# Part of the recurrence's elementwise work on GpSimd and ScalarE in place of VectorE

## The reference

```
xx = shift(h) - h
xr, xw, xk, xv, xa, xg = [h + xx * mix[i] for i in range(6)]
r, k, v = xr @ w_r, xk @ w_k, xv @ w_v
decay = exp(-exp(-softplus(-(w0 + tanh(xw @ w1) @ w2)) - 0.5))
a = sigmoid(a0 + (xa @ a1) @ a2)
kk = k * k_k;  kk = kk / norm(kk, per head)
k = k * (1 + (a - 1) * k_a)
for each token t and each of 16 heads of 64:
    S = S * decay_t - (S kk_t) (kk_t * a_t)^T + v_t k_t^T
    y_t = S r_t
y = group_norm(y) + (sum(r * k * r_k)) * v;  return (y * sigmoid(xg @ g1) @ g2) @ w_o
```

## Time and profile before

| what | value |
| --- | --- |
| timed runs | 2705.49 us median, 2704.85 lowest, 2709.05 highest |
| profiled execution | span 2706.4 us, first to last instruction; no other time is listed for it |
| TensorE busy | 2380.3 us, 88% of the span |
| VectorE busy | 1862.4 us, 69% |
| ScalarE busy | 1218.7 us, 45% |
| GpSimd busy | 622.8 us, 23%, nearly all of it gathers before 1565 us |
| projections of the time mix | end at 2349.3 us |
| triangular inverse | 2386.53 to 2418.83 us |

### The profile page before, as it was taken

How to read it: one execution, slowest core, us unless ns; L and a number is a source line. 1 busy time by engine, 2 the same in 40 slices (tenths; PEclk the granted TensorE clock), 3 DMA queues, 4 the chain that set the end, 5 groups by cost and what they waited for, 6 DMA issues and landing times. The chain is left out here.

```text
span 2706.4 us, 35151 instructions
## 1 busy us (share of the span) xinstructions
PE 2380.3 (88%) x12882; PEld 1586.5 (59%) x12882; DVE 1862.4 (69%) x3462; ACT 1218.7 (45%) x2588; POOL 622.8 (23%) x529
## 2 busy tenths in 40 slices
PE   6988788888888988888778799999999998977999
PEld 4774334333334444343333268898888887866887
DVE  4767866677667867867765666676667666797665
ACT  3433434444444544444434454457445444534543
POOL 0003444554444434455544400000000000000000
PEclk9988999999999999999999999999999998977999
DMA  9789999999999999999999945542555554212553
GB/s 386 257 329 423 403 427 427 424 427 424 424 411 418 376 426 411 427 427 427 427 424 426 427 160 186 186 156 98 183 186 181 188 188 165 91 50 111 179 187 116
DMA packets 121706, 811.27 MB, mean 300 GB/s; under 512 B 15713, under 2 KB 18825, under 8 KB 26584
## 3 DMA queue, kind: packets, MB, share of 16 engines
q0 software_dynamic: 74160, 540.05, 47.7%
q1 hardware_dynamic: 47400, 269.32, 27.5%
HBM read 807.12 MB, written 1.15 MB: 299 GB/s over the span
## 5 line engine op out<-in xcount | busy, mean ns | idle before, releaser
L1402 PE MATMUL bank<-rows,diag 128*128 128x512 f32 (+1 forms) x2060 | 995.9, 620 | 212.6 <-ACT diag L1559 212.1
L1797 DVE CUSTOM_DVE_ANT_0 rows<-rows,h 128x1024 f32<-128x1024 f32 (+1 forms) x512 | 620.3, 1224 | 359.7 <-DMA rows<-in_peer_rows,idx 353.3
L1402 PEld LDWEIGHTS bank<-rows,diag 128*128 128x128 f32 (+1 forms) x2060 | 371.8, 194 | 739.7 <-ACT diag L1559 421.1
L1281 POOL DMA_INDIRECT rows<-in_peer_rows,idx x512 | 609.0, 1189 | 741.5 <-PE bank L1402 679.3
L1550 ACT ACTIVATE picks<-picks 128x1 f32<-128x1 f32 (+1 forms) x512 | 103.3, 202 | 637.9 <-DVE picks L1797 617.5
L2142 PE MATMUL bank<-hT_pair,halves 128*128 128x512 f32 x864 | 307.2, 399 | 0.4 <-DVE hT_pair L2020 0.4
L2143 PE MATMUL bank<-hT_pair,halves 128*128 128x256 f32 x864 | 242.2, 280 | 0.0
L1559 ACT ACTIVATE diag<-const_table,picks 128x128 f32<-128x128 f32 (+1 forms) x512 | 205.5, 401 | 48.0 <-ACT picks L1554 1.1
L2076 DVE TENSOR_TENSOR halves<-weight_ring,halves 128x2048 fp32r<-128x2048 f32 x74 | 169.3, 2289 | 74.3 <-ACT halves L2071 74.1
L2142 PEld LDWEIGHTS bank<-hT_pair,halves 128*128 128x128 f32 x864 | 162.3, 188 | 40.9 <-DVE hT_pair L2020 0.9
L1314 PE MATMUL bank<-halves_b,halves_a 128*128 128x256 f32 x912 | 172.0, 331 | 0.0
(11 more groups left out here) (571 smaller groups left out, 3772.2 us busy)
## 6 DMA issues: line engine op xcount, KB each, us to landing
weight_ring<-in_ffn_w_gate SPq DMA_DIRECT2D x44, 1024.0 KB, 4.7
weight_ring<-in_ffn_w_up SPq DMA_DIRECT2D x44, 1024.0 KB, 4.8
weight_ring<-in_ffn_w_down SPq DMA_DIRECT2D x44, 1024.0 KB, 4.8
mod_ring<-in_mod_w SPq DMA_DIRECT2D x16, 1024.0 KB, 7.5
weight_ring<-in_peer_w_q SPq DMA_DIRECT2D x16, 1024.0 KB, 11.3
half_ring<-in_mod_w SPq DMA_DIRECT2D x24, 512.0 KB, 7.2
rows<-in_mod_w SPq DMA_DIRECT2D x12, 1024.0 KB, 8.1
weight_ring<-in_attn_w_in SPq DMA_DIRECT2D x12, 1024.0 KB, 4.7
```

The source lines that it names most:

```text
L1281: nc.gpsimd.indirect_dma_start(ring[:, s], None, dram["peer_rows"], bass.IndirectOffsetOnAxis(ap=idx[:, T, n:n + 1], axis=0)).then_inc(row ...
L1402: mm = nc.tensor.matmul(bank[:, :], diag[0:n, j % DIAG_SLOTS], ring[0:n, j % ROW_SLOTS, D + half * 512:D + (half + 1) * 512], start=(j in ...
L1797: dotted.up(nc.vector.tensor_tensor_reduce(out=ring[r, s, 0:D], in0=ring[r, s, 0:D], in1=its_h, scale=1.0, scalar=0.0, op0=ALU.mult, op1=A ...
```

## The change

1. In `project_mixes` SP also loads the row k_a (`ka_row`), into the other half of the slot that holds `kk_row`. GpSimd, once both raw removal keys are made, computes for each tile `rated_part = K * ka_row` and `K = K - rated_part`, in that slot.
2. In `wkv` GpSimd multiplies `rated_part` by the rate A, adds it to K, and multiplies K by `down`; VectorE loses `key_factor`, `key` and both products K * down. `rate_key`, which overwrites A, waits for GpSimd's product.
3. VectorE adds the biases of L for both tiles, then those of A.
4. ScalarE copies all grams from PSUM unmasked, between its copies of the turned halves. GpSimd masks GK in SBUF, one instruction for a tile, and then the right half of GA. The inverse reads the left half of GA unmasked, in entries above the diagonal only.
5. The semaphores follow: TensorE's next use of a bank waits for the copy, the products with GK for GpSimd's mask, the shares of GA for the third mask. VectorE's transpose waits for the copies of GA and for GpSimd's K * down, whose input and output it would otherwise overtake.

```
+        @block.gpsimd                       # in project_mixes
+        def _(pool):
+            pool.wait_ge(made.sem, NT)
+            for T in range(NT):
+                kit.pool(nc.gpsimd.tensor_tensor(rated_part[:, T], K[:, T], ka_row, ALU.mult))
+                kit.pool(nc.gpsimd.tensor_tensor(K[:, T], K[:, T], rated_part[:, T], ALU.subtract))
...
+            for T in range(NT):             # in wkv, GpSimd
+                pool.wait_ge(rated.sem, NT + T + 1)
+                key_rated.up(gtt(rated_part[:, T], rated_part[:, T], A[:, T], ALU.mult))
+            for T in range(NT):
+                pool.wait_ge(key_rated.sem, T + 1)
+                kit.pool(gtt(K[:, T], K[:, T], rated_part[:, T], ALU.add))
+                pool.wait_ge(exped.sem, 5 * T + 4)
+                k_scaled.up(gtt(Kd[:, T], K[:, T], down[:, T], ALU.mult))
...
+            pool.wait_ge(rows_in.sem, 32)
+            for T in range(NT):
+                pool.wait_ge(grams_out.sem, 2 * NT + 2 * T + 2)
+                masked.up(mask(GK[:, T * RH:(T + 1) * RH, :], P, 2 * C))
+            masked.up(mask(GA[:, :, C:], P + 3 * C, C))
...
+            place_next(5)                   # in wkv, ScalarE
+            copy_grams(GA, 0, 0)
+            copy_grams(GA, 1, 2)
+            place_next(2)
+            copy_grams(GK, 0, 6)
+            place_next(2)
+            copy_grams(GK, 1, 0)
...
-            key_factor(0)                   # in wkv, VectorE
             rate_key(0)
             scale_r(0)
             scale_keys(0)
-            key_factor(1)
             rate_key(1)
             scale_r(1)
             scale_keys(1)
-            key(0)
             place_half(3)
-            k_scaled.up(tt(Kd[:, 0], K[:, 0], down[:, 0], mul))
-            mask(GA, P + 2 * C, grams_a, masked_a, 0, 0)
-            key(1)
             place_half(4)
             place_half(5)
-            k_scaled.up(tt(Kd[:, 1], K[:, 1], down[:, 1], mul))
-            mask(GA, P + 2 * C, grams_a, masked_a, 1, 2)
+            dve.wait_ge(k_scaled.sem, NT)
+            dve.wait_ge(grams_out.sem, 2 * NT)
...
-                if i in (4, 10):
-                    mask(GK, P, grams_k, masked_k, i // 10, 0 if i == 10 else 6)
```

More of the change, by code:

```diff
@@ L163, in dve, with pool @@
         self.nc.vector.wait_ge(self.step["dve"].sem, self.step["dve"].up(ins))
+    def pool(self, ins):
+        self.nc.gpsimd.wait_ge(self.step["pool"].sem, self.step["pool"].up(ins))
     def act(self, ins):
@@ L3240, in _ @@
         def _(sp):
-            for i, row in enumerate((dram["rw_ka_2"], dram["rw_rk_2"].rearrange("e h d -> e (h d)"))):
-                rows_in.up(sp.dma_start(rows[:, i], bcast(row, D)), 16)
+            rows_in.up(sp.dma_start(rows[:, 1], bcast(dram["rw_rk_2"].rearrange("e h d -> e (h d)"), D)), 16)
             rows_in.up(sp.dma_start(chunks[:], dram["chunks"]), 16)
@@ L3305, in flip, with grams @@
                     turned.up(mm)
-            def grams(T, keys, j, bank, columns_of, done):
+            def grams(T, keys, j, bank, columns_of):
                 for half in range(2):
@@ L3314, in grams @@
                     if hh // 2 == KD - 1:
-                        done.up(mm)
+                        grams_made.up(mm)
             for j in range(4):
                 flip(j)
-            grams(0, BT, 2, 0, first_a, grams_a)
+            grams(0, BT, 2, 0, first_a)
             flip(4)
@@ L3322, in _ @@
             pe.wait_ge(innered.sem, 4)
[L3323 removed]
+            grams(1, BT, 5, 2, first_a)
             flip(6)
[L3325 removed]
+            grams(0, KT, 6, 6, block_of)
             flip(7)
[L3327 to L3330 removed]
+            pe.wait_ge(grams_out.sem, 2)
+            grams(1, KT, 7, 0, block_of)
+            pe.wait_ge(grams_out.sem, 4)
             for q in range(4):
@@ L3501, in _, with copy_grams @@
             exp_before(1)
-            place_next(len(on_act) - 4)
+            def copy_grams(G, T, b):
+                for i in range(2):
+                    act.wait_ge(grams_made.sem, grams_out.n + 1)
+                    grams_out.up(nc.scalar.copy(G[:, T * RH + i:(T + 1) * RH:2, :], kit.bank[b + i][:, :].rearrange("p (a t) -> p a t", t=2 * C)))
+            place_next(5)
[5 more added lines that the diff above has]
+            copy_grams(GK, 1, 0)
             for T in range(NT):
@@ L3554, in _ @@
             tt, stt = nc.vector.tensor_tensor, nc.vector.scalar_tensor_tensor
[L3555 to L3559, removed]
             def place_half(j):
@@ L3565, in _ @@
             dve.wait_ge(bias_in.sem, 32)
-            for T in range(NT):
-                for m, dst in enumerate((L, A)):
+            for m, dst in enumerate((L, A)):
+                for T in range(NT):
                     for i in range(2):
@@ L3577, in _ @@
                     biased.up(tt(quarter(before, 2 * T + i), kit.bank[4 + 2 * T + i][:, :], quarter(L, 2 * T + i), ALU.subtract))
[L3578 to L3585, removed]
+            dve.wait_ge(rows_in.sem, 32)
             def rate_key(T):
+                dve.wait_ge(key_rated.sem, T + 1)
                 step(tt(A[:, T], A[:, T], KN[:, T], mul))
@@ L3748, in _, with mask @@
             cleared.up(nc.gpsimd.memset(slot(4)[:, 0:C * C:C + 1], 1.0))
+            gtt = nc.gpsimd.tensor_tensor
+            for T in range(NT):
[6 more added lines that the diff above has]
+                k_scaled.up(gtt(Kd[:, T], K[:, T], down[:, T], ALU.mult))
+            def mask(G, at, n):
+                return gtt(G, G, chunks[:, at:at + n].unsqueeze(1).to_broadcast([P, G.shape[1], n]), ALU.mult)
+            pool.wait_ge(rows_in.sem, 32)
+            for T in range(NT):
+                pool.wait_ge(grams_out.sem, 2 * NT + 2 * T + 2)
+                masked.up(mask(GK[:, T * RH:(T + 1) * RH, :], P, 2 * C))
+            masked.up(mask(GA[:, :, C:], P + 3 * C, C))
             pool.wait_ge(within_out.sem, 4 * NT)
```

18 lines of the change are left out of this document (11 added, 7 removed).

## The result

The changed kernel took 2718.93 us in the median of seven runs (2716.83 to 2720.26), the kernel before 2709.05 in the median of seven beside it (2704.85 to 2714.43). The ratio is 1.0036, with a 95% interval of 1.0025 to 1.0046: slower by 9.9 us. A second group of five runs later gave 2720.23 against 2707.87, ratio 1.0049 (1.0035 to 1.0063).

What follows compares the result with a forecast made beforehand. VectorE was taken as the bound up to the triangular inverse's end. Projections +3.4 and the inverse's end +10.4 (its start +5.3 included) gave +13.8: span 2706.4 to 2720.2, less 0.9, 2719 us (2713 to 2725; 8 in 10: 2704 to 2725).

Steps and rivals of the forecast that it cites:

- What bounds the kernel, and the sign: VectorE bounds up to the triangular inverse's end; holds in turns (chance 0.62) make the change slower (chance 0.72).
- signs that it named: VectorE instructions at 3 us and more, GpSimd's at 3.7, projections' block ending 3 late, three inverse steps stretched by 2.5.
- What it costs VectorE: A VectorE instruction with two SBUF inputs waits out GpSimd's whole tensor-tensor of 2.5 us; bounds were nothing and 2.5.
- Projections' last block: Four GpSimd instructions of 2.5 us alternate with VectorE's split and normalisations; the block's end waits, +3.4 us.
- Low-rank products: TensorE's products after the projections: no term in the sum; a little lower TensorE clock stood only in the range's upper end.
- Ahead of the inverse: Scaling of the keys: first product 2.4 late, four GpSimd slips +10.0, two key factors gone -2.5; ends 9.9 later.
- Up to the inverse's start: From second scaled r through turns and grams: the inverse starts at 2391.8 in place of 2386.53, +5.3.
- The inverse: Two mask pairs leave its 32.3 us, three GpSimd masks hold VectorE 3 x 2.5: 37.4 us, ending +10.4.
- VectorE never held: Rival, chance 0.19: only GpSimd waits; inverse starts and ends 7.5 earlier, own-chunk states limit the gain to -4.9, 2700.6 us.
- second path: Last copies of own-chunk states, 0.6 us behind the inverse; without holds they end at 2414.0, limiting the gain to -4.9.
- Both slowed: Rival, chance 0.12: both engines slow while they meet; at two thirds speed +1.5, 2707 us; at half speed +9.
- VectorE wins every turn: Rival, chance 0.07: GpSimd's first mask waits for the inverse's end; +15, and +3 at the projections, 2724 us.

Runs made afterwards that it cites:

- The clears: Changed kernel with each of GpSimd's thirteen two-input instructions replaced by three write-only clears, values of k and masks lost; 2700.99 us, ratio 0.9975 to the kernel before.
- first half only: Kernel before with only K * ka_row and K - rated_part on GpSimd, rest of k on VectorE; 2.4 us at the block's end, 2.9 in low-rank products.
- the pair of 4.81: In the kernel before plus six idle-time pairings: four two-input VectorE instructions beside a GpSimd tensor-tensor, 1.94 us more than the 2.87 beside a clear.
- the probe: Kernel before plus six pairings in VectorE's idle time, each four VectorE instructions of 512 columns beside one GpSimd instruction of 1024; 2731.09 us, one run.

## Why the prediction was right

The forecast was 2719 and the median is 2718.93, but that closeness is largely luck. The forecast was a change of +13.5 us on a kernel before of 2705.49; beside the changed kernel that one took 2709.05 in seven runs, and the change was +9.9. And within the sum errors cancel: by stages of the first profile the holds were priced 4.0 us too dear in three stages, and the low-rank products and the turn stage came out 4.6 us dearer than reckoned.

*What bounds the kernel, and the sign.* Right. VectorE's path set the end of the inverse, before and after. The step that decided, that the hold works in both directions and in turns, was the one trusted least, and it was taken from gathers that showed only one direction. (The trace of before shows a little of the other direction too, which the prediction's median of 1225 ns hides: in the eight cases in which a gather starts within 0.02 us of VectorE's multiplication, the gather takes 0.94, unheld, and the multiplication 1.24 to 1.28.) The clears show it by the opposite: without the reads the same program is 6.4 us faster by stages than before, with them 12.7 to 14.4 slower. Of the signs that it named, VectorE's instructions are at 3.25 to 3.37 (3 and more), each ending about one VectorE length after a GpSimd one; GpSimd's own are at 3.2 to 3.3, not 3.7; VectorE ends the block 2.4 after the last copy of V, not 3; the three steps are 2.0 longer, not 2.5.

*What GpSimd gets.* 2.5 us was estimated for an instruction, measured 2.34 to 2.49 over all profiles. *What it costs VectorE.* The whole 2.5 was taken; measured 2.01 to 2.15 in eight places, about 0.35 less than GpSimd's own length: VectorE's instruction begins up to 0.3 us into GpSimd's, and is let go 0.14 before its end. This is the term that was mis-sized. It shows at every place where it stood:

*Projections' last block.* Predicted +3.4, measured +2.44: the split is 1.15 longer and the two normalisations 3.60, together 4.75; 2.3 of it went unnoticed, since VectorE had ended 2.6 us ahead of the first low-rank product and now ends 0.3 ahead.

*Low-rank products.* Predicted nothing, measured +2.93 and, in another execution, +1.69. The prediction reckoned with "TensorE's clock, a little lower for its longer wait" only as an end of its range; the block's late end of 2.4 costs 1.7 to 2.9 more. This term was missing from the sum.

*Ahead of the inverse.* Predicted +9.9 (a late start of 2.4, four holds of 2.5, two key factors gone), measured +8.34: the same five holds, 10.45 in all, less 2.5, and 0.4 ahead of the first of them: from the first bias to the first scaled key it is 8.03 in place of 7.63, with two waits of 0.17 for TensorE between the biases of L, which now come first. A kernel with the old order of the biases (first half only) has 7.63 again.

*Up to the inverse's start.* The prediction's +5.3 over both stages means -4.6 in the turn stage; measured -2.98 and -3.54. The reason is TensorE's clock again. While VectorE is held, TensorE waits for it (busy 5.36 of the 10 us up to 2375), and after a wait of 3.86 it runs at the lower level: from 2375.0 to 2386.0 of the changed kernel the clock is 0.50, where the earlier trace rows has 1.00 for the same work. The window, and TensorE's rows from that wait on:

```profile
2375.00:2386.00 11.00, 6.54 (x76) 5.42 (x78) 10.93 (x7) 5.27 (x10) 5.92 (x2) 0.50 0.00 1
```

```profile
2372.25 1.97 PE L3317 MATMUL bank<-const_table,R 128*128 128x128 f32 x8 [3.86 <-DVE R L3606]
...
2383.39 1.97 PE L3317 MATMUL bank<-const_table,R 128*128 128x128 f32 x8 [2.58 <-DVE R L3606]
2385.29 2.06 PE L3325 MATMUL bank<-arT,hT 64*32 64x64 f32 x128
2387.28 1.88 PE L3317 MATMUL bank<-const_table,weight_ring 128*128 128x128 f32 x8
...
2391.47 1.48 PE L3325 MATMUL bank<-arT,turned_keys 64*32 64x64 f32 x128 [0.88 <-DVE arT L3235]
```

The prediction's path from the second scaled r to the inverse can be set against them term by term. The turn and the first grams were taken from rows at the higher level, 1.1 + 1.5, and take 4.0 (2383.33 to 2387.35); two turns with their copies 4.0 in place of 3.4; the second grams, taken from a row at the lower level (2.04) and now at the higher one, 1.6 with the wait ahead of them; ScalarE's copies 1.15 in place of 1.1. Together 10.8 in place of 9.1, which is the 1.6 us missing. In the second profile the level is back earlier, the eight turns behind the grams take 1.32 in place of 1.88, and the stage is shorter by the same 0.56:

```profile
2386.63 1.32 PE L3317 MATMUL bank<-const_table,weight_ring 128*128 128x128 f32 x8
```

*The inverse.* Predicted +5.1 (three holds of 7.5 less 2.4), measured +3.64: 6.10 less 2.42, which is 3.68.

*The sum.* Predicted 13.8, measured 14.37 and 12.67 by stages. The timed differences, 9.9 and 12.4, lie below both; the first profile of the change had its raw keys 3.2 us earlier than before's, with one more row load as the only changed work ahead of them, so that its span grew by 10.7 only. How much of the gap between 9.9 and 12.7 is such spread and how much is chance in two medians stays open.

*The rivals.* "VectorE never held" was priced at -4.9, limited by the own-chunk states; the clears show -6.4 for a kernel without holds, in which GpSimd doesn't wait either, so that second path did not bind as reckoned (states stays 9.56). It is close: the last copies of the own-chunk states end at 2413.43, the inverse at 2413.55. "Both slowed", +1.5, falls with the pair of 4.81 and the eight holds: a two-input instruction is either at 1.22 or longer by what is left of GpSimd's. "VectorE wins every turn" falls with the alternation in the first two timelines.

## What to carry to other kernels

Moving elementwise work to an idle GpSimd can pay only beside VectorE work that neither reads two operands from SBUF nor copies within SBUF. Beside two-input work each tensor-tensor of 1024 columns (2.4 us) cost VectorE 2.0 to 2.15, more than the 1.22 that it saved; beside biases read from PSUM, a transpose or idle time it cost nothing, and there the gain was small too (0.7 us for five instructions, by stages). So go by what stands opposite it in VectorE's timeline, not by GpSimd's idle share. And where a block's end slips, ask what TensorE's longer wait does to its clock: here 2.4 us of slip brought 1.7 to 2.9 more.

## What the runs showed of the hardware that was not expected

- A held VectorE instruction takes its own length from 0.14 us ahead of the recorded end of GpSimd's (0.13 to 0.15 in the eight places and the probe). Queued on both engines, that makes 2.01 to 2.15 us for a GpSimd tensor-tensor of 2.4, and in the probe 0.74 for a copy of 1.04; a clear of 0.95 holds two-input work for nothing.
- A copy of 512 columns from SBUF to SBUF on VectorE, 0.43 by itself, took 2.48 beside a GpSimd tensor-tensor and 1.13 beside a clear.
- A wait for the other engine is recorded as busy time of the waiting instruction (3.37 for 1.22, 3.32 for 2.4), so busy shares rise with contention.
- After a wait of 3.34 or 3.36 us TensorE ran at the lower level for 6.0 us in one execution and 3.7 in another (products of 0.63 in place of 0.38).
- Extra products that kept the level up once, at 5.79, were followed in their one profile by a lower level some 45 us later, where the last stage took 4.78 more; they had won 2.93.
